# A two-layer decoder trunk: the last three weight blocks ahead of each norm by token half, the norms filled by token half, and GpSimd's rescale in 512-column pieces

## The chip, the core and the metric

The kernel runs on one core of one Trainium2 chip. The metric is the device time of one execution in microseconds (us). The core has five engines with a queue each: TensorE (PE in the profile; its weight loads are PEld), VectorE (DVE), ScalarE (ACT), GpSimd (POOL) and SyncE (SP, which issues the loads). An engine takes its instructions in the order in which they are written; semaphores order the engines against each other.

## What is computed

Two post-norm layers over 256 tokens of 2048 features, in float32. Layer 0 mixes with retention and pooling, layer 1 with sliding-window attention; each is followed by a convolutional gated feed-forward (FFN), and each half ends in a layer norm:

```python
for layer in range(DEPTH):                       # DEPTH = 2
    mix = retention_pool_mixer(...) if layer % 2 == 0 else swa_sink_attention(...)
    x = layer_norm(DEEPNORM_ALPHA * x + mix, ln_gain[layer, 0], ln_bias[layer, 0])
    ffn = conv_glu_ffn(x, ffn_w_in[layer], ffn_conv_w[layer], ffn_conv_b[layer], ffn_w_out[layer])
    x = layer_norm(DEEPNORM_ALPHA * x + ffn, ln_gain[layer, 1], ln_bias[layer, 1])
```

There are four norms: norm 0 (ahead of the FFN of layer 0), norm 1 (ahead of the attention's input projection), norm 2 (ahead of the FFN of layer 1) and the last one, which makes the output. A norm needs mean and variance over all 2048 features of a token, and different tokens do not meet in it.

## The kernel before

**Blocks.** All large products run over 356 weight blocks of 512 x 512 (4 tiles of 128 rows, 512 columns), numbered by `s`. SyncE loads a block into `raw` (4 buffers), ScalarE rounds it to `w_hi` (`high(s)`, L455, 4 buffers), VectorE makes the rest `w_lo = raw - w_hi` (`low(s)`, L698, 3 buffers), and TensorE multiplies. When TensorE has finished a block it counts `used` up. `low(s)` waits until block `s - 3` is used up, `high(s)` until block `s - 4` is. The activations stand as `T` in the same two parts (256 tokens high, 256 low). A product is written one of two ways: turned (`turned_mm`, L1099 and L1100: the weight tile is stationary, tokens stream; 64 pairs of one 512-column and one 256-column matmul for four blocks) or plain (`plain_tile`, L1116 to L1118: 128 tokens are stationary and 512 weight columns stream; 12 matmuls for a token half of a block, 24 for a block).

**Up to a norm.** The last projection of a stage is plain: for each block both token halves `a = 0, 1`, 12 matmuls each. After the last block VectorE adds the result to the residual `xres` (`add_last`, L739), takes statistics (L745, L750), ScalarE the square root (L502), VectorE the reciprocal, and then normalises `xres` in eight pieces of 512 columns (L768: four column quarters, two token halves).

**The fill.** The next product needs the normalised rows turned: TensorE transposes two feature tiles for both token halves (`turn_pair`, L1128, four transposes, two pairs a quarter), ScalarE applies gain and bias and writes `half` (L482, twice) and then the high part of `T` (L487), VectorE writes the low part (L758, `fill_normed_low`) and counts `t_ready`. There are eight such pairs for a norm. `first_chunk` on TensorE turns quarter 0, and then, between the two parts of each block's product, the whole quarter that the next block needs. A part is the product with two feature tiles: 8 pairs of matmuls. "Chunk 0" below is the first four blocks after a norm, "chunk 1" the next four, `base` the first block's number.

**The rescale.** The residual needs gain, bias and the factor alpha as well. GpSimd waits until the eighth pair is turned (`turned`) and then runs four instructions of 2048 columns on `xres`: two multiplications (L428) and two additions (L431). Later residual additions, the load of the next norm's parameters, and in the attention the reuse of the parameters' buffer wait for its count `scaled`.

**Chunk 1 of an FFN.** VectorE's queue holds `low(base+5)`, `low(base+6)`, a small copy, a convolution of two feature tiles (a sum of a PSUM tile and `half`, L719; two scalings, L890; four multiply-adds, L893, all of 256 columns a tile), `low(base+7)`, a second such convolution, `low(base+8)`, `low(base+9)`. Chunk 1 of the attention has the lows and a few small instructions on the keys and values.

**The end.** The last norm (L788 to L805) is divided among VectorE, ScalarE and GpSimd after the last matmul; five transfers store the output (L395 to L403).

Of the kernel before, what the change touches and what calls it, by code (L numbers as in the profile page):

```python
# [20 lines left out]
F32 = mybir.dt.float32  # L21
F32R = mybir.dt.float32r
ALU = mybir.AluOpType
# [48 lines left out]
S_FFN = [S_FFN0, S_FFN1]  # L72

FILL_X, FILL_RET, FILL_LN0, FILL_LN1, FILL_ATT, FILL_LN2 = 0, 8, 12, 20, 28, 36
FILL_LN = [FILL_LN0, FILL_LN1, FILL_LN2]
ATT_FILL_BANKS = [2, 3, 2, 3, 4, 5, 4, 5]
ATT_FILL_AT = {0: 0, 1: 2, 4: 4, 6: 6}

SPLIT_AFTER = {1: 0, 5: 1, 7: 2}
# [43 lines left out]
def build_trunk(nc, x, ln_gain, ln_bias, even_w_in, pool_w, pool_scale, even_w_out, attn_w_qkv, attn_b_qkv,  # L125
# [10 lines left out]
    with ExitStack() as ctx:  # L136
# [142 lines left out]

        ret_bank = lambda hd: 4 + hd % 2  # L280
# [5 lines left out]
        def _(sp):  # L286
# [30 lines left out]
            def ffn(l):  # L317
# [6 lines left out]
                sp.wait_ge(scaled, TOK * (2 * l + 2))  # L324
# [68 lines left out]
            for q in range(2):  # L393
                sp.wait_ge(last_first, q + 1)
                sp.dma_start(out_t[:, 0, cols(2 * q * COLS, 2 * COLS)], xres[:, 0, cols(2 * q * COLS, 2 * COLS)]) \  # L395
                    .then_inc(stored, 16)
            sp.wait_ge(last_second, 1)
            sp.dma_start(out_t[:, 1, cols((NCH - 1) * COLS)], xres[:, 1, cols((NCH - 1) * COLS)]) \
                .then_inc(stored, 16)
            for n0, n1 in ((0, NCH - 2), (NCH - 2, NCH - 1)):  # L400
                c = slice(COLS * n0, COLS * n1)
                sp.wait_ge(last_scaled, n1)
                sp.dma_start(out_t[:, 1, c], xres[:, 1, c]).then_inc(stored, 16)  # L403
# [4 lines left out]
        def _(pool):  # L408
# [11 lines left out]
            for m in range(3):  # L420

                pool.wait_ge(lnp_landed, 32 * (m + 1))
                nc.gpsimd.tensor_scalar(lnp, lnp, ALPHA, 1.0, ALU.mult, ALU.mult).then_inc(pool_step, 1)
                pool.wait_ge(turned, FILL_LN[m] + 8)
# [7 lines left out]
                steps += TOK  # L432
# [13 lines left out]
        def _(act):  # L446
# [26 lines left out]
            def fill_normed(m, s):  # L473

                for j in range(8):
                    n = FILL_LN[m] + j
                    act.wait_ge(turned, n + 1)
                    if j >= 2:
                        act.wait_ge(t_ready, n - 1)
                    for t in range(2):  # L480
                        c = KT * m + 2 * j + t
                        ins = nc.scalar.activation(half[:, n % 2, t], ps[:, fill_bank(n), SEQ * t:SEQ * t + SEQ],  # L482
# [3 lines left out]
                    act.wait_ge(act_step, 8 * m + j + 1)  # L486
                    nc.scalar.activation(T[:, 2 * j:2 * j + 2, 0:SEQ], half[:, n % 2], ACT.Copy).then_inc(t_hi, 1)  # L487
                    if j in SPLIT_AFTER:
                        high(s + HI_LEAD + SPLIT_AFTER[j])

# [9 lines left out]
            def ln_root(m):  # L500
                act.wait_ge(var_ready, m + 2)
                nc.scalar.activation(rstd[:], rstd[:], ACT.Sqrt).then_inc(std_ready, 1)  # L502
# [71 lines left out]
            for s in range(S_EVEN_OUT, S_FFN0):  # L574
                high(s + HI_LEAD)
# [12 lines left out]
            def feed_forward(l):  # L588
                base, tp, gp = S_FFN[l], TP_FFN[l], 2 * FC * l
                ln_root(2 * l)  # L590
# [26 lines left out]
                for j in range(16):  # L617
# [30 lines left out]
            ln_root(1)  # L648
            fill_normed(1, S_ODD_IN)
            for s in range(S_ODD_IN + 1, S_FFN1):  # L650
# [19 lines left out]
            ln_root(3)  # L670

            act.wait_ge(shift_ready, 1)
            for n in range(NCH):
                c = slice(COLS * n, COLS * n + COLS)
                nc.scalar.activation(xres[:, 1, c], xres[:, 1, c], ACT.Identity, bias=shift[:], scale=rstd[:, 1:2]) \
                    .then_inc(last_normed, 1)


        @block.vector
        def _(dve):  # L680
# [49 lines left out]
            def add_last(m, bank, count_in, ended):  # L730

                n = NCH - 1
                c = slice(COLS * n, COLS * n + COLS)
                for a in range(TOK):
                    if a == 0:
                        dve.wait_ge(last_half, m + 1)
                    else:
                        dve.wait_ge(used, ended)
                    ins = vec.tensor_tensor(xres[:, a, c], xres[:, a, c], ps[:, bank + a], ALU.add)  # L739
                    if a == TOK - 1:  # L740
                        ins.then_inc(count_in[0], 1)
                        dve.wait_ge(*count_in)
                    else:
                        chain(ins)
                    ins = vec.bn_stats(stats[:, a, n], xres[:, a, c])  # L745
                chain(ins)

            def inverse_root(m):
                for a in range(TOK):
                    ins = vec.bn_aggr(mean_var[:, a], stats[:, a])  # L750
                chain(ins)
                vec.tensor_scalar(rstd[:], mean_var[:, :, 1], EPS, None, ALU.add).then_inc(var_ready, 1)
                dve.wait_ge(std_ready, m + 2)
                chain(vec.reciprocal(rstd[:], rstd[:]))

            def fill_normed_low(n, j):
                dve.wait_ge(t_hi, n + 1)
                vec.tensor_tensor(T[:, 2 * j:2 * j + 2, SEQ:2 * SEQ], half[:, n % 2],  # L758
                                  T[:, 2 * j:2 * j + 2, 0:SEQ].bitcast(F32), ALU.subtract).then_inc(t_ready, 1)

            def layer_norm(m, s):

                inverse_root(m)

                def normalise(q):
                    for a in range(TOK):
                        c = slice(COLS * q, COLS * q + COLS)
                        ins = vec.tensor_scalar(xres[:, a, c], xres[:, a, c], mean_var[:, a, 0:1],  # L768
                                                rstd[:, a:a + 1], ALU.subtract, ALU.mult)
                    ins.then_inc(ln_chunk, 1)  # L770

                for q in range(3):
                    normalise(q)
                for j in range(8):
                    fill_normed_low(FILL_LN[m] + j, j)
                    if j == 0:
                        normalise(3)
                    if j == 1 and m == 1:
                        low(s + LO_LEAD - 1)
                    if j in SPLIT_AFTER:  # L780
# [707 lines left out]
```

## Time and profile before

| | us |
|---|---|
| median of three runs | 2164.05 (2163.34 to 2165.15) |
| span of the profiled execution | 2162.8 |
| TensorE busy | 2097.6 (97%) |
| VectorE busy | 1455.7 (67%) |
| ScalarE busy | 902.5 (42%) |
| GpSimd busy | 90.6 (4%) |
| mean granted TensorE clock | 0.985 of full speed |

The span is the profiled execution from its first to its last instruction, 1.25 us less than the median of the timed runs. Busy time is a sum over an engine's instructions; TensorE's matmuls overlap at their ends. PEclk is the granted TensorE clock as a share of the full 2.4 GHz, so 0.50 is 1.2 GHz. A row of a timeline that ends in x2 stands for two instructions one after the other, with their time from the first start to the last end.

### The profile page before, as it was taken

Reading aid. Unit: us, or ns where it says so; the run is one execution under the profiler, and the core shown is the slowest. Engines: PE = TensorE matmul, PEld = TensorE weight load, DVE = VectorE, ACT = ScalarE, POOL = GpSimd, SP = SyncE. Lnnn points to the kernel's source line nnn. Section 1 sums busy time; section 2 is a strip of 40 time slices with the busy share of each in tenths; the row PEclk is TensorE's granted clock in tenths of the full one; section 3 lists DMA queues with packets and bytes.
Section 4 is the critical chain, followed back from the end, with each engine's and each line's share of the span. In section 5 each row is a group of like instructions: output and inputs, shape, how many; then the busy total and the mean of one; then the engine's idle time right before and its main releaser. Section 6 shows DMA issues by size and latency. Waiting matters only on the chain.

```text
span 2162.8 us, 27677 instructions
## 1 busy us (share of the span) xinstructions
PE 2097.6 (97%) x10996; PEld 1788.2 (83%) x10996; DVE 1455.7 (67%) x1564; ACT 902.5 (42%) x852; POOL 90.6 (4%) x29
## 2 busy tenths in 40 slices
PE   8999998999999999999989999989999999999996
PEld 7888887788888888888877888778888888888885
DVE  5434455967766667767777666586776767767677
ACT  4443435434433434434443554444343334434341
POOL 0000000200000000000003000030000000000001
PEclk9999999999999999999999999999999999999998
DMA  8664373565555555555544335446555555555551
GB/s 303 221 194 156 114 260 133 196 206 183 192 178 192 193 191 178 193 191 180 176 160 161 118 117 179 153 156 233 179 189 194 180 190 193 175 195 193 192 178 58
DMA packets 194077, 390.39 MB, mean 180 GB/s; under 512 B 6409, under 2 KB 8803, under 8 KB 192995
## 3 DMA queue, kind: packets, MB, share of 16 engines
q1 hardware_dynamic: 193731, 389.31, 53.7%
q8 instruction: 42, 0.69, 0.1%
q10 hardware_dynamic: 288, 0.26, 0.1%
q14 instruction: 16, 0.13, 0.0%
HBM read 387.18 MB, written 2.10 MB: 180 GB/s over the span
## 4 chain that ended last, share of the span: by engine, by line
PE 95%; DVE 3%; ACT 1%; issue 0%; DMA 0%; DVEq 0%; ACTq 0%
PE ps L1099 36%; PE ps L1100 18%; PE ps L1116 12%; PE ps L1118 12%; PE ps L1117 12%; DVE w_lo L698 1%; DVE T L758 1%; PE ps L1128 1%; PE ps L1382 1%; PE ps L1365 0%; PE ps L1247 0%; DVE xres L798 0%; ACT w_hi L455 0%; PE ps L1358 0%; PE ps L1356 0%
## 5 line engine op out<-in xcount | busy, mean ns | idle before, releaser
L1099 PE MATMUL ps<-T,w_hi 128*128 128x512 f32 x3360 | 1205.9, 403 | 26.0 <-DVE T L758 13.9
L698 DVE TENSOR_TENSOR w_lo<-raw,w_hi 128x2048 fp32r<-128x2048 f32 x355 | 839.9, 2368 | 460.8 <-PE ps L1100 350.2
L455 ACT ACTIVATE w_hi<-raw 128x2048 fp32r<-128x2048 f32 x355 | 680.7, 1919 | 1041.9 <-PE ps L1100 626.2
L1100 PE MATMUL ps<-T,w_lo 128*128 128x256 f32 x3360 | 951.3, 283 | 0.0
L1099 PEld LDWEIGHTS ps<-T,w_hi 128*128 128x128 f32 x3360 | 640.0, 190 | 188.2 <-DVE T L758 17.0
L1100 PEld LDWEIGHTS ps<-T,w_lo 128*128 128x128 f32 x3360 | 644.2, 192 | 0.7
L1116 PE MATMUL ps<-w_hi,gT 128*128 128x512 f32 x672 | 262.3, 390 | 0.0
L1118 PE MATMUL ps<-w_hi,gT 128*128 128x512 f32 x672 | 262.0, 390 | 0.0
L1117 PE MATMUL ps<-w_lo,gT 128*128 128x512 f32 x672 | 261.8, 390 | 0.0
L1116 PE MATMUL ps<-w_hi,T 128*128 128x512 f32 (+1 forms) x512 | 199.0, 389 | 0.7 <-DVE T L712 0.7
L1118 PE MATMUL ps<-w_hi,T 128*128 128x512 f32 (+1 forms) x512 | 197.0, 385 | 0.0
L1117 PE MATMUL ps<-w_lo,T 128*128 128x512 f32 (+1 forms) x512 | 196.9, 385 | 0.0
L893 DVE SCALAR_TENSOR_TENSOR arena<-arena,cur 128x256 f32<-128x256 f32 x352 | 155.1, 482 | 6.3
L724 DVE TENSOR_TENSOR xres<-xres,ps 128x1024 f32<-128x1024 f32 x92 | 112.0, 1218 | 70.0 <-PE ps L1118 69.9
L1118 PEld LDWEIGHTS ps<-w_hi,gT 128*128 128x128 f32 x672 | 126.2, 188 | 26.7
L1116 PEld LDWEIGHTS ps<-w_hi,gT 128*128 128x128 f32 x672 | 126.2, 188 | 26.4
L1117 PEld LDWEIGHTS ps<-w_lo,gT 128*128 128x128 f32 x672 | 126.2, 188 | 25.6
L1116 PEld LDWEIGHTS ps<-w_hi,T 128*128 128x128 f32 x512 | 97.2, 190 | 21.5 <-issue 1.3
L1118 PEld LDWEIGHTS ps<-w_hi,T 128*128 128x128 f32 x512 | 97.0, 190 | 19.0
L1117 PEld LDWEIGHTS ps<-w_lo,T 128*128 128x128 f32 x512 | 97.1, 190 | 18.2
L719 DVE TENSOR_TENSOR arena<-ps,half 128x512 f32<-128x512 f32 x96 | 65.7, 688 | 17.3 <-ACT half L497 12.1
L890 DVE TENSOR_SCALAR arena<-arena,cur 128x256 f32<-128x256 f32 x176 | 64.7, 410 | 3.2
(126 smaller groups left out, 811.9 us busy)
## 6 DMA issues: line engine op xcount, KB each, us to landing
raw<-ffn_w_in SPq DMA_DIRECT2D x176, 1024.0 KB, 5.0
raw<-ffn_w_out SPq DMA_DIRECT2D x88, 1024.0 KB, 5.0
raw<-even_w_in SPq DMA_DIRECT2D x39, 1024.0 KB, 5.2
raw<-attn_w_qkv SPq DMA_DIRECT2D x20, 1024.0 KB, 5.2
raw<-even_w_out SPq DMA_DIRECT2D x16, 1024.0 KB, 5.1
raw<-attn_w_out SPq DMA_DIRECT2D x16, 1024.0 KB, 5.0
arena<-ln_gain SPq DMA_DIRECT2D x4, 1024.0 KB, 7.2
arena<-ln_bias SPq DMA_DIRECT2D x4, 1024.0 KB, 9.2
```

Source lines behind the costliest of these rows:

```text
L455: nc.scalar.activation(w_hi[:, s % HI], raw[:, s % RAW], ACT.Copy).then_inc(hi_ready, 1)
L698: vec.tensor_tensor(w_lo[:, s % LO], raw[:, s % RAW], w_hi[:, s % HI].bitcast(F32), ALU.subtract).then_inc(lo_ready, 1)
L719: vec.tensor_tensor(to, ps[:, bank:bank + 2, 0:SEQ], half[:, n % 2], ALU.add).then_inc(added, 1)
L724: vec.tensor_tensor(xres[:, :, c], xres[:, :, c], ps[:, bank:bank + 2], ALU.add).then_inc(count_in, 1)
L758: vec.tensor_tensor(T[:, 2 * j:2 * j + 2, SEQ:2 * SEQ], half[:, n % 2], T[:, 2 * j:2 * j + 2, 0:SEQ].bitcast(F32), ALU.subtract).then_inc( ...
L890: ins = vec.tensor_scalar(conv[:, i], h[:, i, 0:SEQ], cur[:, kind, 0, i:i + 1], cur[:, kind, 3, i:i + 1], ALU.mult, ALU.add)
L893: ins = vec.scalar_tensor_tensor(conv[:, i], h[:, i, k:k + SEQ], cur[:, kind, k, i:i + 1], conv[:, i], ALU.mult, ALU.add)
L1099: mm(ps[:, bank], w_hi[:, s % HI, k, c], T[:, t], start=kg == 0 and k == 0, stop=False)
L1100: return mm(ps[:, bank, 0:SEQ], w_lo[:, s % LO, k, c], T[:, t, 0:SEQ], start=False, stop=kg == KG - 1 and k == GK - 1)
L1116: mm(ps[:, bank, 0:n], x_hi, w_hi[:, s % HI, k, c], start=start and k == 0, stop=False)
L1117: mm(ps[:, bank, 0:n], x_hi, w_lo[:, s % LO, k, c], start=False, stop=False)
L1118: ins = mm(ps[:, bank, 0:n], x_lo, w_hi[:, s % HI, k, c], start=False, stop=stop and k == GK - 1)
```

## The change

- **Ends by token half.** The last three blocks ahead of each norm (`ENDS = 3`) run for tokens 0 to 127 first (`ends_first`), then for 128 to 255 (`ends_second`). `used` is counted only in the second pass. Norms 0 to 2 put the transposes of three units of the first half between the matmuls of the second pass.
- **Norm by token half.** VectorE adds, takes statistics and normalises the first half (`first_half_norm`), then the second (`second_half_norm`).
- **Fill in 12 units** (`LN_UNITS`): three of four tiles of half 0, eight of two tiles of half 1, and the last four tiles of half 0 as unit 7. A unit of half 1 has two transposes where a pair had four. `norm_chunk` takes the place of `first_chunk` for the norms.
- **Rescale.** GpSimd runs 16 instructions of 512 columns instead of four of 2048, and waits for `used` to reach `SCALE_AFTER` too: the end of chunk 0 for the two FFNs, two blocks into chunk 0 for the attention. The scaling of the parameters goes from one instruction to four.
- **The last norm.** The first half is normed during the second pass, half of its columns by ScalarE and GpSimd; the second half by VectorE alone, and the stores follow in that order.

The core of the diff:

```diff
+SCALE_AFTER = [S_FFN0 + KG, S_ODD_IN + 2, S_FFN1 + KG]
+LN_UNITS = [(0, 0, 4), (0, 4, 8), (0, 8, 12), (1, 0, 2), (1, 2, 4), (1, 4, 6), (1, 6, 8), (0, 12, 16),
+            (1, 8, 10), (1, 10, 12), (1, 12, 14), (1, 14, 16)]
+PAIR_UNIT = [3, 4, 5, 6, 8, 9, 10, 11]
+END_TURNS = {4: 0, 5: 1, 7: 2}
-SPLIT_AFTER = {1: 0, 5: 1, 7: 2}
+BLOCK_AFTER = {4: 1, 6: 2, 9: 3, 11: 4}
...
-                for a in range(TOK):
-                    nc.gpsimd.tensor_tensor(xres[:, a], xres[:, a], lnp[:, 0], ALU.mult).then_inc(pool_step, 1)
-                for a in range(TOK):
-                    pool.wait_ge(pool_step, steps + a + 1)
-                    nc.gpsimd.tensor_tensor(xres[:, a], xres[:, a], lnp[:, 1], ALU.add).then_inc(scaled, 1)
+                pool.wait_ge(turned, FILL_LN[m] + LN_FILLS)
+                pool.wait_ge(used, SCALE_AFTER[m])
+                pieces = [(a, slice(COLS * n, COLS * n + COLS)) for a in range(TOK) for n in range(NCH)]
+                for a, c in pieces:
+                    nc.gpsimd.tensor_tensor(xres[:, a, c], xres[:, a, c], lnp[:, 0, c], ALU.mult) \
+                        .then_inc(pool_step, 1)
+                for a, c in pieces:
+                    steps += 1
+                    pool.wait_ge(pool_step, steps)
+                    nc.gpsimd.tensor_tensor(xres[:, a, c], xres[:, a, c], lnp[:, 1, c], ALU.add).then_inc(scaled, 1)
...
+            def second_half_norm(m, s):
+                variance(m, 1)
+                inverse_root(m, 1)
+                normalise(1, 0)
+                fill_normed_low(m, 2)
+                for q in range(1, NCH):
+                    normalise(1, q)
+                for u in range(3, LN_FILLS):
+                    fill_normed_low(m, u)
+                    if u in BLOCK_AFTER:
+                        low(s + BLOCK_AFTER[u])
...
+            def norm_chunk(s0, m, product):
+                first = FILL_LN[m]
+                turn_unit(m, 3)
+                turn_unit(m, 4)
+                for j in range(8):
+                    kg, part = divmod(j, 2)
+                    pe.wait_ge(t_ready, first + PAIR_UNIT[j] + 1)
+                    if part == 0:
+                        ready(s0 + kg)
+                    for k in (2 * part, 2 * part + 1):
+                        ins = product(s0 + kg, kg, k)
+                    if part == 1:
+                        ins.then_inc(used, 1)
+                    if 5 + j < LN_FILLS:
+                        turn_unit(m, 5 + j)
```

**TensorE, chunk 0 after norm 0, before.** L1128 are the transposes of a quarter, L1099 and L1100 the matmul pairs of the product. The quarter that is turned here is needed from the row that waits for `lo_ready,t_ready`.

```order
L1128 MATMUL ps<-ident,xres 128x128 [waits t_ready,ln_chunk]
L1128 MATMUL ps<-ident,xres 128x128 x7
L1099 MATMUL ps<-T,w_hi 128x512 [waits t_ready]
L1100 MATMUL ps<-T,w_lo 128x256
...
L1099 MATMUL ps<-T,w_hi 128x512 [waits lo_ready,t_ready]
```

Between the transposes and the first matmul that needs them stand the eight pairs of one part.

**TensorE, the same chunk, after**: L1214 are a unit's transposes, L1147 and L1148 the pairs. The first two rows here are unit 8, then comes part 4, then unit 9, then part 5.

```order
L1214 MATMUL ps<-ident,xres 128x128 [waits t_hi,ln_chunk]
L1214 MATMUL ps<-ident,xres 128x128
L1147 MATMUL ps<-T,w_hi 128x512 [waits lo_ready,t_ready]
L1148 MATMUL ps<-T,w_lo 128x256
...
L1214 MATMUL ps<-ident,xres 128x128 [waits t_hi,ln_chunk]
L1214 MATMUL ps<-ident,xres 128x128
L1147 MATMUL ps<-T,w_hi 128x512 [waits t_ready]
L1148 MATMUL ps<-T,w_lo 128x256
```

By `PAIR_UNIT` parts 4 to 7 wait for units 8 to 11, and each of these is turned right behind the part before: nothing stands between a unit's transposes and the matmul that waits for it. Units 5 and 6 have a part between.

**VectorE, the end of the fill and the head of chunk 1, after.** L779 are low parts of `T`, L719 is `low` (from `low(base+3)` on), L740, L910 and L913 the convolution. The order of these instructions is that of before.

```order
L719 TENSOR_TENSOR w_lo<-raw,w_hi 128x2048 [waits used,hi_ready]
L779 TENSOR_TENSOR T<-half,T 128x2x128 [waits t_hi] x2
L719 TENSOR_TENSOR w_lo<-raw,w_hi 128x2048 [waits used,hi_ready]
L924 MEMSET arena 128x4x2
L719 TENSOR_TENSOR w_lo<-raw,w_hi 128x2048 [waits used,hi_ready,dve_step]
L719 TENSOR_TENSOR w_lo<-raw,w_hi 128x2048 [waits used,hi_ready]
L928 COPY cur<-taps 128x16
L740 TENSOR_TENSOR arena<-ps,half 128x2x256 [waits half_out,dve_step]
L910 TENSOR_SCALAR arena<-arena,cur 128x256 [waits added]
L910 TENSOR_SCALAR arena<-arena,cur 128x256
L913 SCALAR_TENSOR_TENSOR arena<-arena,cur 128x256 [waits dve_step]
```

What moved is the unit before `low(base+4)`: it is now the unit that TensorE's last part of chunk 0 waits for.

**GpSimd, the rescale of norm 0, after.**

```order
L443 TENSOR_TENSOR xres<-xres,arena 128x512 [waits pool_step,used,turned]
L443 TENSOR_TENSOR xres<-xres,arena 128x512 x7
L448 TENSOR_TENSOR xres<-xres,arena 128x512 [waits pool_step] x8
```

The first piece now waits for `used` as well; before, `turned` alone let it go.

## Rows read from the trace of the kernel before

**Rows 1.** The page's groups: `low` and `high` (busy us, mean ns, idle before).

```profile
L698 DVE TENSOR_TENSOR w_lo<-raw,w_hi 128x2048 fp32r<-128x2048 f32 x355 | 839.9, 2368 | 460.8 <-PE ps L1100 350.2
L455 ACT ACTIVATE w_hi<-raw 128x2048 fp32r<-128x2048 f32 x355 | 680.7, 1919 | 1041.9 <-PE ps L1100 626.2
```

**Rows 2.** TensorE's waits, whole run: for whom, us in total, times, longest.

```profile
PE ps L1099 <- DVE T L758: 13.9, 9, 2.5
PE ps L1128 <- DVE xres L768: 10.8, 3, 3.6
PE ps L1099 <- DVE w_lo L698: 10.8, 3, 3.6
```

**Rows 3.** Busy time by stretch, norms 0 and 1, and the end (length, engines, PEclk, DMA, GB/s).

```profile
341.60:347.00 5.40, 5.37 (x24) 4.13 (x22) 3.67 (x3) 3.21 (x2) 0.00 (x0) 1.00 0.58 195
347.00:354.20 7.20, 1.98 (x9) 1.58 (x9) 5.68 (x14) 2.64 (x6) 0.00 (x0) 0.64 0.18 71
354.20:359.30 5.10, 5.10 (x16) 4.33 (x17) 3.71 (x4) 2.56 (x3) 0.00 (x0) 0.50 0.11 12
...
373.30:386.60 13.30, 10.31 (x48) 8.05 (x47) 12.00 (x3) 6.38 (x8) 13.23 (x3) 0.87 0.24 79
386.60:390.20 3.60, 0.00 (x0) 0.01 (x1) 3.56 (x3) 2.88 (x3) 3.60 (x2) 0.97 0.00 0
390.20:393.40 3.20, 3.18 (x10) 2.72 (x11) 3.20 (x1) 0.00 (x0) 3.20 (x1) 0.50 0.67 207
...
1148.50:1154.60 6.10, 6.07 (x19) 5.23 (x20) 6.10 (x1) 0.00 (x0) 4.31 (x1) 0.50 0.51 172
...
2142.70:2162.80 20.10, 0.00 (x0) 0.00 (x0) 14.82 (x17) 3.13 (x5) 9.56 (x6) 0.63 0.26 104
```

**Rows 4.** Timeline of TensorE, norm 0 (start, length, instruction, idle before).

```profile
350.58 1.97 PE L1128 MATMUL ps<-ident,xres 128*128 128x128 f32 x8 [3.61 <-DVE xres L768]
...
371.55 0.39 PE L1099 MATMUL ps<-T,w_hi 128*128 128x512 f32 x1
...
371.89 0.40 PE L1099 MATMUL ps<-T,w_hi 128*128 128x512 f32 x1
...
372.24 1.04 PE L1128 MATMUL ps<-ident,xres 128*128 128x128 f32 x8
```

**Rows 5.** Timeline of VectorE and ScalarE behind the last matmul of norm 0.

```profile
349.52 2.82 DVE L768 TENSOR_SCALAR xres<-xres,mean_var,rstd 128x512 f32<-128x512 f32 x6
...
351.73 1.02 ACT L482 ACTIVATE half<-ps,ln_cols 128x256 f32<-128x256 f32 x2 [2.44 <-PE ps L1128]
352.78 0.63 ACT L487 ACTIVATE T<-half 128x512 fp32r<-128x512 f32 x1
...
353.44 0.69 DVE L758 TENSOR_TENSOR T<-half,T 128x512 fp32r<-128x512 f32 x1 [1.10 <-ACT T L487]
```

**Rows 6.** Timeline of GpSimd during the rescale of norm 0.

```profile
373.37 9.57 POOL L428 TENSOR_TENSOR xres<-xres,arena 128x2048 f32<-128x2048 f32 x2 [95.47 <-PE ps L1128]
382.90 11.61 POOL L431 TENSOR_TENSOR xres<-xres,arena 128x2048 f32<-128x2048 f32 x2
```

**Rows 7.** The same stretch on VectorE.

```profile
374.60 8.89 DVE L758 TENSOR_TENSOR T<-half,T 128x512 fp32r<-128x512 f32 x2 [1.96 <-ACT T L487]
383.41 6.66 DVE L698 TENSOR_TENSOR w_lo<-raw,w_hi 128x2048 fp32r<-128x2048 f32 x1
```

**Rows 8.** The end: pieces of 512 columns on GpSimd.

```profile
2149.48 1.71 POOL L439 TENSOR_TENSOR xres<-xres,arena 128x512 f32<-128x512 f32 x1
...
2152.82 1.71 POOL L439 TENSOR_TENSOR xres<-xres,arena 128x512 f32<-128x512 f32 x1
```

**Rows 9.** The last two stores on SyncE's queue.

```profile
2158.47 0.94 SPq L403 DMA_DIRECT2D out<-xres  x2
```

**Rows 10.** TensorE alone in two stretches (busy, PEclk, DMA share, GB/s).

```profile
1270.60:1274.00 3.40, 2.09 (x19) 1.00 0.89 280
...
345.60:349.00 3.40, 1.37 (x7) 1.00 0.77 283
```

More of the change, by code:

```diff
@@ L748, in inverse_root @@
[L748 to L780, printed above, removed]
-                        low(s + LO_LEAD + SPLIT_AFTER[j])
@@ L956, in feed_forward @@
                 tail, c = base + FFN_GROUPS - 4 * KG, FC - 1
-                for j in range(16):
+                for j in range(13):
                     if j == 11:
@@ L1160, in first_chunk, with turn_unit @@
                     ins.then_inc(used, 1)
+            def turn_unit(m, u):
+                a, t0, t1 = LN_UNITS[u]
+                n = FILL_LN[m] + u
+                pe.wait_ge(ln_chunk, TOK * NCH * m + NCH * a + t0 // KG + 1)
+                if u >= 4:
+                    pe.wait_ge(t_hi, n - 3)
+                for t in range(t0, t1):
+                    i = t - t0
+                    ins = nc.tensor.transpose(ps[:, fill_bank(n), P * i:P * i + P], xres[:, a, P * t:P * t + P],
+                                              ident[:])
+                ins.then_inc(turned, 1)
@@ new lines, in ends_first, with ends_second @@
+            def ends_first(blocks, each):
+                for s, src, tile, bank, start, stop in blocks:
+                    ready(s)
+                    ins = plain_tile(s, src, tile, bank, 0, start, stop)
+                    if each or stop and s == blocks[-1][0]:
+                        ins.then_inc(last_half, 1)
+            def ends_second(blocks, m):
+                for i, (s, src, tile, bank, start, stop) in enumerate(blocks):
+                    for k in range(GK):
+                        ins = plain_tile(s, src, tile, bank + 1, 1, start, stop, only=k)
+                        if k == GK - 1:
+                            ins.then_inc(used, 1)
+                        if m is not None and GK * i + k in END_TURNS:
+                            turn_unit(m, END_TURNS[GK * i + k])
@@ L1259, in projection @@
                     ins = plain_tile(s, gT if in_g else T, 0 if in_g else GK * kg, bank + a, a, first, last)
-                    if a == 0 and last and n == NCH - 1:
-                        ins.then_inc(last_half, 1)
                 ins.then_inc(used, 1)
-            for i in range(NCH * KG):
+            for i in range(NCH * KG - ENDS):
                 s, n, pos = S_EVEN_OUT + i, i // KG, i % KG
@@ L1438, in _ @@
                 scores(b)
+            ends = [(S_FFN1 - ENDS + i, T, GK * (1 + i), ODD_OUT_BANKS[-1], False, i == ENDS - 1)
+                    for i in range(ENDS)]
+            ends_first(ends, False)
+            ends_second(ends, 2)
             feed_forward(1)
```

301 lines of the change are left out of this document (179 added, 122 removed).

## The prediction, made before the changed kernel was run

> **What bounds the kernel now.** TensorE is busy 97% of the span, so time goes where it waits or runs at half clock. I read its waits first [rows 2], then a table of stretches around the norms [rows 3], then the timelines there. The three norms 0 to 2 look alike. Behind the last matmul TensorE has nothing for 3.6 us, does eight transposes and waits again; the first matmul comes after 7.2 us [rows 3, 4]. Near the end of chunk 0 it loses 3.0 us (13.30 less 10.31 busy) and at the head of chunk 1 another 3.6, 10.8 over the three norms [rows 2, 3]. After each such hole the granted clock is 0.50, so that 5.1 us behind the norm give half their work, and 3.2 (norm 0) or 6.1 (norm 1) at chunk 1 [rows 3]. At the end 20.1 us pass without a matmul [rows 3].
>
> The two later holes come from GpSimd. While its four instructions run (21.2 us together), one `low` lasts 6.66 us instead of 2.3, and two small fills 8.89 together instead of 1.4 [rows 1, 5 to 7]: the two engines take turns, an instruction each. Take out what VectorE did in between, two fills and a `low`. VectorE's pace is (2.37 - 0.69)/1536 = 1.1 ns a column [rows 1, 5], so 0.56 for 512 columns, 2.2 for 2048, 0.28 for 256. That leaves 21.2 - 3.3 = 17.9 us of GpSimd's own, **1.11 us for 512 columns**. The end agrees: two pieces and two VectorE instructions of 512 in 3.34 us [rows 8], 1.67 - 0.56 = 1.11.
>
> **The change part by part.** The sum runs from the last three blocks to the end of chunk 1, norm by norm. Paces: 12 plain matmuls take 2.7 us (24 in 5.40, rows 3), a turned pair 0.345 [rows 4], so a part 2.8, a block 5.5, a chunk 22.1; a transpose takes 0.13 [rows 4].
>
> *Ends.* The matmuls are the same. Three blocks' first halves take 8.2 us, the last `low` among them starts with the first of them and is needed 5.4 us later: it fits. Twelve transposes go in (+1.56) and eight fewer stand in chunk 0 (-1.04): +0.5 a norm, **+1.6**. The first half's add, statistics and norm (2.5 + 1.9, rows 3 and 5), the next `low` and two fills fit the 9.7 us of the second pass; TensorE covers them.
>
> *The gap.* Behind the last matmul VectorE still adds, takes statistics and normalises one piece: 3.0 us instead of 3.6 [rows 4, 5]. Four transposes at half clock take 1.0. VectorE meanwhile has a fill (0.69) and three pieces (1.4) and then the first unit's low part (0.42): first matmul at 5.6. Against 7.2 that is 1.6 less at norms 0 and 2. At norm 1 VectorE's queue also holds the second half's other two adds and statistics, one pair of them behind a `low`, so that the last add starts 1.2 us late: 6.8, which I count as no gain. **-3.2** together. I found no reason for the half clock behind it to shorten: the hole is still above 4 us, and 1.37 us busy of 3.4 was followed by 0.50, 2.09 of 3.4 was not [rows 10].
>
> *Round trips in chunk 0.* Parts 4 to 7 wait for a unit turned just ahead of them. ScalarE writes two tiles (1.02 for 256 columns each, rows 5; its pace is (1.92 - 0.63)/1536 = 0.84 ns a column [rows 1, 5], so 0.81) and copies 256 columns (0.42), VectorE subtracts (0.42), and four hand-overs take 0.2: 1.85 us in which TensorE is idle. Halving all of today's trip gives 1.4, all of it 2.6. I take 1.85: the parts have rows. Four a norm, twelve in all: **+22.2** (16 to 31). Nothing covers them. Before, a part (2.8 us) stood between, and there was no wait.
>
> *Clock there.* Holes of 1.85 between parts of 2.8. In 3.4 us that leaves about 1.4 us busy, close to the stretch that was followed by half clock [rows 10]. I take one fall a norm at the price seen in chunk 0 today, 0.87 over 13.3 us, that is 1.7 us: **+5.1** (0 to 15).
>
> *Rescale out of chunk 0.* Its 3.0 us of waits and 1.7 of clock go: **-14.0** for three norms. Its waits at chunk 1's head go too, 10.8, and their clock, 1.6 at norm 0 and 3.0 at norms 1 and 2: **-18.4**.
>
> *Rescale in chunk 1 (norms 0 and 2).* GpSimd's 16 pieces are 17.9 us, now from the end of chunk 0. Four blocks later, at 22.1 us, TensorE needs `low(base+8)`. Ahead of it on VectorE stand: the rest of `low(base+4)` (0.9, since the unit before it comes late: ScalarE's 1.9 us and the 2.3 of `low` start 0.5 us before the last part, which lasts 2.8), four lows (8.8), four scalings, a copy (together 0.8) and eight multiply-adds (2.2). With strict turns each of these 16 or 17 lets a piece in, so all 16 pieces come first: 17.9 + 12.7 = 30.6 less 22.1 is 8.5; I take 8.1, some of VectorE's starts overlapping. TensorE waits at `base+4` (0.9), `base+7` (2.5) and `base+8` (4.7). Twice: **+16.2**. Clock: two falls, 1.7 and 2.3: **+8**. Bounds: if only instructions known to wait count (two inputs in SBUF), 12 pieces get in and 3.7 us are left a norm; if GpSimd gets few turns, only the 0.9.
>
> The Trainium skill, SBUF — State Buffer, "Who interferes with whom", says that one read and write port pair is shared, is held for the whole instruction, and that two-port forms of tensor_scalar and copy take it as well as two-input instructions. The turns agree with [rows 6, 7]; that the scalings count no run here shows. By it 16 pieces come ahead.
>
> *Norm 1.* The rescale may start two blocks into chunk 0, so `turned` lets it go, with the last unit's transposes, 4.6 us ahead of the end of chunk 0. The second piece stands ahead of that unit's fill (0.95 more), and turns make `low(base+4)` and `low(base+6)` late by 0.7 together. There is no convolution, so a low meets one piece and fits into a block: 2.2 + 1.1 of 5.5. `scaled` is complete some 31 us after the start, about 3 us behind the eighth block. VectorE waits there, and TensorE's first scores need what stands behind that wait 5.5 us after the eighth block: covered by half a microsecond. **+1.7**; if that cover goes, 1 to 3 more.
>
> *End.* Before, 20.1 us [rows 3]. After: the first half's add starts 8.2 us before the last matmul, its statistics and root take 2.5, and its four instructions of 512 columns 2.8 and, since GpSimd's four pieces take turns with them, 1 to 2 more; behind them two adds with statistics of 1.45 each. So VectorE comes to the last add 2.0 us after the last matmul. From there 2.5 to the first normed piece, eight instructions of 512 columns at 0.69 [rows 5] 5.5, and one store; today the last store starts 3.9 us before the span's end (2158.47 and half of 0.94, against 2162.8) [rows 9]. 2.0 + 2.5 + 5.5 + 3.9 = 13.9: **-6.2**. If GpSimd's turns cost nothing it is 12, if they cost twice as much 15.5.
>
> Sum: +1.6 - 3.2 + 22.2 + 5.1 - 14.0 - 18.4 + 16.2 + 8 + 1.7 - 6.2 = **+13.0**. The span becomes 2162.8 + 13.0 = 2175.8; it stands 1.25 under the median before, and I keep that: 2177.
>
> **The rivals.** *Faster: turns without a price in chunk 1.* If VectorE's short instructions pass in groups and GpSimd fits its pieces into VectorE's other time, 7.2 us of the 8.1 and the 4 of clock go at each FFN norm: 13.0 - 22.4 = -9.4, 2155. It decides when fewer than 9 pieces stand ahead of `low(base+8)`: 12.7 + 8.5 x 1.11 = 22.1. For it: nothing is known of turns with 0.3 us instructions. Against it: every pair in [rows 6 to 8] alternates. *Half of that:* scalings and copy do not take a turn, 12 pieces: 13.0 - 8.8 - 4 = 0, 2164. *Round trips hidden:* if the order of transposes did not bind, 27.3 go: 2150. The order of the queue speaks against it. *Slower still: the clock.* If TensorE falls to 1.2 GHz after most of the round trips, three falls a norm, +10: 2187. The Trainium skill, TensorE: Matmul & The Clock Gate, "Part 4: PE-mode transpose", says that transposes do not count as busy; the clock was 0.50 during the eight in the gap [rows 3, 4], which does not separate the causes. By that rule this rival gains.
>
> **How the numbers follow.** Forecast (2169 to 2183) 0.55; slower still 0.11; half 0.10; no price in chunk 1 0.15; trips hidden or another gain 0.09. Slower by over 0.2% (4.3 us, about what a measurement of this kernel can tell) 0.66, within 0.11, faster 0.23. The range leaves out the 0.09 and part of the two ends: 2154 to 2187.
>
> **What would show it.** In chunk 0, four holes of 1.85 us a norm before L1147 for `T`; in chunk 1 of the FFNs, waits of L1147 for `w_lo` of 8 us together while GpSimd's pieces last 1.4 to 3.3 us each; no such waits in chunk 0; a first matmul 5.6 us after a norm; 14 us after the last matmul. If the holes in chunk 0 are missing the forecast is wrong by 27 us; if `w_lo` is in time in chunk 1, by 22.

## The result

Four runs of each kernel, timed in turns.

| | before | after |
|---|---|---|
| median, us | 2163.7 (2163.0 to 2165.15) | 2180.84 (2179.83 to 2181.58) |
| ratio after / before, 95% interval | | 1.0074 (1.0062 to 1.0085) |
| span of the profiled execution, us | 2162.8 | 2178.9 |

The change makes the kernel 0.7% slower: 17.1 us by the medians, 16.1 by the spans. 2177 was predicted, in a range of 2154 to 2187, slower with a chance of 0.66. The time between the last matmuls of the stages, read from TensorE's timeline:

| stage, us | before | after | difference |
|---|---|---|---|
| start to norm 0 | 346.97 | 347.63 | +0.7 |
| norm 0 to norm 1 (FFN) | 758.8 | 769.7 | +10.9 |
| norm 1 to norm 2 (attention) | 277.0 | 280.3 | +3.2 |
| norm 2 to the last matmul (FFN) | 759.9 | 768.8 | +8.9 |
| behind the last matmul | 20.1 | 12.5 | -7.6 |

### The profile page after: what moved, and what is told of

Read it like the earlier page. It is cut to its first block, busy times and chain, and to the rows that moved or that the text cites. A ratio compares the mean times of both kernels' runs of the same rounds, so it can differ in the third digit from the quotient of the medians.

```text
span 2178.9 us, 27743 instructions
## 1 busy us (share of the span) xinstructions
PE 2106.8 (97%) x10996; PEld 1792.2 (82%) x10996; DVE 1445.1 (66%) x1590; ACT 915.9 (42%) x914; POOL 115.8 (5%) x72
## 4 chain that ended last, share of the span: by engine, by line
PE 92%; DVE 5%; ACT 1%; issue 1%; DMA 0%; DVEq 0%; ACTq 0%
PE ps L1147 35%; PE ps L1148 18%; PE ps L1164 12%; PE ps L1166 12%; PE ps L1165 12%; DVE w_lo L719 1%; DVE arena L913 1%; PE ps L1481 1%; ACT half L500 0%; DVE T L779 0%; PE ps L1464 0%; PE ps L1214 0%; PE ps L1176 0%; DVE arena L910 0%; DVE xres L772 0%
## 5 line engine op out<-in xcount | busy, mean ns | idle before, releaser
L1147 PE MATMUL ps<-T,w_hi 128*128 128x512 f32 x3360 | 1213.1, 405 | 41.7 <-DVE T L779 27.4
L719 DVE TENSOR_TENSOR w_lo<-raw,w_hi 128x2048 fp32r<-128x2048 f32 x355 | 823.8, 2323 | 459.9 <-PE ps L1148 342.2
L1148 PE MATMUL ps<-T,w_lo 128*128 128x256 f32 x3360 | 952.1, 283 | 0.0
L1147 PEld LDWEIGHTS ps<-T,w_hi 128*128 128x128 f32 x3360 | 642.5, 191 | 207.5 <-DVE T L779 31.2
L1148 PEld LDWEIGHTS ps<-T,w_lo 128*128 128x128 f32 x3360 | 645.7, 192 | 0.7
L913 DVE SCALAR_TENSOR_TENSOR arena<-arena,cur 128x256 f32<-128x256 f32 x352 | 170.6, 526 | 6.3
L745 DVE TENSOR_TENSOR xres<-xres,ps 128x1024 f32<-128x1024 f32 x88 | 107.1, 1218 | 60.8 <-PE ps L1166 60.8
L443 POOL TENSOR_TENSOR xres<-xres,arena 128x512 f32<-128x512 f32 x24 | 42.5, 1802 | 901.5 <-PE ps L1214 707.3
L740 DVE TENSOR_TENSOR arena<-ps,half 128x512 f32<-128x512 f32 x96 | 65.7, 688 | 17.6 <-ACT half L517 12.5
```

The lines of the kernel that those rows point to most:

```text
L443: nc.gpsimd.tensor_tensor(xres[:, a, c], xres[:, a, c], lnp[:, 0, c], ALU.mult) \
L719: vec.tensor_tensor(w_lo[:, s % LO], raw[:, s % RAW], w_hi[:, s % HI].bitcast(F32), ALU.subtract).then_inc(lo_ready, 1)
L740: vec.tensor_tensor(to, ps[:, bank:bank + 2, 0:SEQ], half[:, n % 2], ALU.add).then_inc(added, 1)
L745: vec.tensor_tensor(xres[:, :, c], xres[:, :, c], ps[:, bank:bank + 2], ALU.add).then_inc(count_in, 1)
L913: ins = vec.scalar_tensor_tensor(conv[:, i], h[:, i, k:k + SEQ], cur[:, kind, k, i:i + 1], conv[:, i], ALU.mult, ALU.add)
L1147: mm(ps[:, bank], w_hi[:, s % HI, k, c], T[:, t], start=kg == 0 and k == 0, stop=False)
```

## The profile after

The page, engines: busy us, share, instructions.

```profile
span 2178.9 us, 27743 instructions
PE 2106.8 (97%) x10996; PEld 1792.2 (82%) x10996; DVE 1445.1 (66%) x1590; ACT 915.9 (42%) x914; POOL 115.8 (5%) x72
```

TensorE is as busy in share as before. Busy time hides what matters here: it grew by 9.2 us with the same matmuls, 7.5 of them because more of it is at half clock (the account below). GpSimd's busy time grew by 25 us. The rescale has the same columns and is 23 of these; a part of that is waiting for its turn inside an instruction.

TensorE's waits in the whole run, as [rows 2].

```profile
PE ps L1147 <- DVE T L779: 27.4, 15, 2.9
PE ps L1147 <- DVE w_lo L719: 13.0, 4, 5.7
PE ps L1214 <- DVE xres L772: 9.7, 3, 3.7
```

The wait for `T` has doubled (13.9 before), that for `w_lo` has grown a little (10.8 before) and has another place. By stretch, as [rows 3]: the gap behind norm 0 and what follows it; a round trip; three stretches of 3.4 us in chunk 0; then chunk 1, its large hole and what follows it; the last trip of norm 1; the end.

```profile
347.60:352.90 5.30, 0.95 (x5) 0.53 (x4) 4.82 (x11) 2.52 (x7) 0.00 (x0) 0.81 0.27 106
352.90:357.70 4.80, 4.76 (x15) 4.08 (x16) 2.71 (x2) 2.45 (x3) 0.00 (x0) 0.50 0.00 0
367.70:369.50 1.80, 0.00 (x0) 0.00 (x1) 0.42 (x1) 1.22 (x3) 0.00 (x0) 1.00 0.80 188
374.80:378.20 3.40, 3.40 (x11) 2.92 (x12) 2.26 (x1) 1.11 (x1) 0.00 (x0) 0.50 0.00 0
381.60:385.00 3.40, 3.40 (x12) 2.90 (x11) 0.00 (x0) 0.00 (x0) 0.00 (x0) 0.50 0.32 122
388.40:391.80 3.40, 3.40 (x13) 2.93 (x12) 2.51 (x3) 3.40 (x3) 0.00 (x0) 0.50 0.00 0
392.70:416.10 23.40, 22.41 (x128) 19.06 (x126) 23.15 (x17) 8.53 (x8) 23.40 (x14) 1.00 0.52 179
416.10:421.70 5.60, 0.00 (x1) 0.00 (x0) 5.60 (x4) 3.26 (x3) 3.43 (x3) 0.77 0.00 0
421.70:426.00 4.30, 4.26 (x13) 3.68 (x14) 4.30 (x2) 1.94 (x3) 0.00 (x0) 0.50 0.74 239
1157.00:1159.90 2.90, 0.03 (x1) 0.00 (x0) 1.53 (x1) 2.80 (x4) 2.78 (x3) 0.99 0.00 0
2166.40:2178.90 12.50, 0.00 (x0) 0.00 (x0) 9.15 (x16) 0.20 (x1) 1.53 (x2) 0.65 0.42 167
```

Read it in four steps. The gap is 5.3 us instead of 7.2. The third row is one of the round trips: nothing on TensorE while ScalarE and VectorE make the unit. The three rows at 0.50 are matmuls at 1.2 GHz inside chunk 0, busy 3.40 of 3.40, at a clock that lets through half of the work. In chunk 1 there is a hole of 5.6 us in which VectorE is busy throughout, and 4.3 us at half clock behind it.

One round trip on TensorE, ScalarE and VectorE (the timeline: start, length, instruction, idle before):

```profile
372.44 0.38 PE L1214 MATMUL ps<-ident,xres 128*128 128x128 f32 x2
372.86 0.81 ACT L500 ACTIVATE half<-ps,ln_cols 128x128 f32<-128x128 f32 x2 [3.87 <-PE ps L1214]
373.69 0.42 ACT L505 ACTIVATE T<-half 128x256 fp32r<-128x256 f32 x1
374.14 0.43 DVE L779 TENSOR_TENSOR T<-half,T 128x256 fp32r<-128x256 f32 x1 [4.70 <-ACT T L505]
374.62 0.68 PE L1147 MATMUL ps<-T,w_hi 128*128 128x512 f32 x1 [1.80 <-DVE T L779]
```

0.81, 0.42 and 0.43 of work and 0.14 in hand-overs are the 1.80 us in which TensorE is idle. Eleven of the twelve trips read 1.80 or 1.81; the last one of norm 1 reads 2.91, where GpSimd runs already.

The head of chunk 1 on GpSimd, VectorE and TensorE, norm 0:

```profile
392.69 13.85 POOL L443 TENSOR_TENSOR xres<-xres,arena 128x512 f32<-128x512 f32 x8 [114.99 <-PE ps L1148]
397.13 1.26 DVE L928 COPY cur<-taps 128x16 f32<-128x16 f32 x1
399.15 1.93 DVE L910 TENSOR_SCALAR arena<-arena,cur 128x256 f32<-128x256 f32 x2
401.11 5.71 DVE L913 SCALAR_TENSOR_TENSOR arena<-arena,cur 128x256 f32<-128x256 f32 x4
406.50 13.03 POOL L448 TENSOR_TENSOR xres<-xres,arena 128x512 f32<-128x512 f32 x8
406.75 3.38 DVE L719 TENSOR_TENSOR w_lo<-raw,w_hi 128x2048 fp32r<-128x2048 f32 x1
412.75 5.65 DVE L913 SCALAR_TENSOR_TENSOR arena<-arena,cur 128x256 f32<-128x256 f32 x4
418.33 5.55 DVE L719 TENSOR_TENSOR w_lo<-raw,w_hi 128x2048 fp32r<-128x2048 f32 x2
421.74 0.79 PE L1147 MATMUL ps<-T,w_hi 128*128 128x512 f32 x1 [5.63 <-DVE w_lo L719]
```

and the same small instructions of VectorE before, at that place, where GpSimd had nothing to do:

```profile
398.79 0.16 DVE L909 COPY cur<-taps 128x16 f32<-128x16 f32 x1
399.71 0.74 DVE L890 TENSOR_SCALAR arena<-arena,cur 128x256 f32<-128x256 f32 x2
400.49 1.80 DVE L893 SCALAR_TENSOR_TENSOR arena<-arena,cur 128x256 f32<-128x256 f32 x4
```

A multiply-add takes 1.4 instead of 0.45 us, a copy of 16 columns 1.26 instead of 0.16. Each lets one whole GpSimd piece in, short or long. The two sums that read a PSUM tile (L740) do not: they take 0.69 and 0.68 us among the pieces, and 0.69 where GpSimd has nothing to do. The 16th piece starts just ahead of `low(base+8)` (418.09 and 418.33), so all 16 pieces delay it, as the prediction had it for strict turns. The Trainium skill, SBUF — State Buffer, "Who interferes with whom", names copy and tensor_scalar, in their two-port forms, among the instructions that take the shared port pair: the trace agrees (1.26 us for the copy, 0.97 as the mean of two scalings).

The end: the last residual add, and the last stores.

```profile
2168.07 0.67 DVE L754 TENSOR_TENSOR xres<-xres,ps 128x512 f32<-128x512 f32 x1
2173.32 3.11 SPq L412 DMA_DIRECT2D out<-xres  x3
```

**An account.** Summing TensorE's rows up to the last matmul gives its idle time, its time busy at half clock, and (busy less half of that) its work in microseconds at full clock. The loss by the clock is half the time at half clock. "Behind" is the time from the last matmul to the end of the span.

| up to the last matmul, us | idle | at half clock | loss by the clock | work at full clock | behind |
|---|---|---|---|---|---|
| before | 45.1 | 42.3 | 21.2 | 2076.5 | 20.1 |
| after | 59.6 | 57.3 | 28.7 | 2078.1 | 12.5 |
| difference | +14.5 | | +7.5 | +1.7 | -7.6 |

## The experiments

Theory: two causes of loss, the round trips with the clock they bring, and the rescale in chunk 1, whose delay is set by the number of turns; the end gives some back. The rivals: the clock would be low anyway; the lateness in chunk 1 comes from columns or from the order on VectorE, not from turns; the late start of the rescale is harmless. Each ratio below is against the kernel before on the same chip, with its 95% interval.

### e1: each unit turned one part earlier

```diff
                     if part == 0:
                         ready(s0 + kg)
+                    if 5 + j < LN_FILLS:
+                        turn_unit(m, 5 + j)
                     for k in (2 * part, 2 * part + 1):
                         ins = product(s0 + kg, kg, k)
...
-                    if 5 + j < LN_FILLS:
-                        turn_unit(m, 5 + j)
```

> The changed kernel with one thing moved: in chunk 0 each unit's transposes stand ahead of a part's product, not behind it, so that a part of 2.8 us lies between them and the matmul that needs them. If the round trips are what costs: the twelve holes of 1.8 us go (21.7 us, and the 1.1 more at norm 1), and with them the nine stretches at half clock inside chunk 0 (about 15 us); the hole in chunk 1 grows by 1 to 2 us a norm, since the rescale then starts earlier against the same queue. 2180.8 - 38 + 3 = 2146. Rival, that the half clock in chunk 0 comes from the transposes or from the gap behind the norm and not from the holes: the falls stay, 2160. Rival, that something else (ScalarE's fills) sets the pace of chunk 0: above 2170.

Measured: 2143.15 us, ratio 0.9904 (0.9888 to 0.9921), 37.7 less than after. The account: idle 38.4, at half clock 26.4, work 2077.1. So 21.2 us of idle time and 15.5 of clock went. The stretch that read 0.79 in after:

```profile
372.00:388.00 16.00, 16.00 (x93) 13.67 (x92) 12.69 (x11) 12.07 (x12) 8.16 (x4) 1.00 0.67 225
```

TensorE's waits:

```profile
PE ps L1147 <- DVE w_lo L719: 14.9, 5, 5.6
PE ps L1214 <- DVE T L779: 4.3, 3, 1.5
```

The waits of the product for `T` have gone; what stays of them is one wait of the transposes a norm. The large hole in chunk 1 is as in after (5.63 at norm 0) and the small one has grown from 0.99 to 1.65, so the two causes are nearly separate. This single move turns the loss into a gain.

### e9: transposes in the holes, to part the trip from its clock

Behind the transposes of each of the four units eight more transposes, of `ident`, go to a PSUM bank that is free; nobody reads them. Nothing is left out.

```diff
+                    if j in (3, 4, 5, 6):
+                        n = first + 5 + j
+                        pe.wait_ge(t_hi, n - 2)
+                        for i in range(8):
+                            nc.tensor.transpose(ps[:, 4 + (n + 1) % 4, P * (i % 4):P * (i % 4) + P],
+                                                ident[:], ident[:])
```

> The changed kernel with eight more transposes of the identity (1.0 us) in each of the four holes of 1.8 us of a chunk 0, so that TensorE is idle for 0.8 us there; when the product goes on is unchanged. Nothing reads what they write. If they keep the clock at 2.4 GHz: the nine stretches at half clock inside chunk 0 go, 2180.8 - 15 = 2166. If transposes do not count for the clock: the falls stay, 2181. Either way the waits for T remain, only their idle share shrinks.

Measured: 2168.47 us, ratio 1.002 (1.001 to 1.003), 12.4 less than after with 96 matmuls more. The stretch around three trips, after and then e9:

```profile
372.00:388.00 16.00, 10.59 (x43) 8.57 (x41) 3.57 (x4) 6.05 (x11) 0.00 (x0) 0.79 0.21 66
```

```profile
372.00:388.00 16.00, 12.78 (x80) 10.71 (x78) 5.72 (x5) 9.46 (x13) 0.28 (x1) 1.00 0.20 66
```

All nine stretches at half clock in chunk 0 are gone: 57.3 us at half clock became 27.4 in the whole run, a gain of 15.0 us. The trips are as long as before; 0.93 us of each is still idle. The kernel gains less than 15, since the 96 transposes add 13.2 us of work and fill only 11.1 of idle time. So of the 37.7 us of e1 some 15 were the clock and the rest the trips themselves. And the transposes did hold the clock up: that speaks against the sentence of the Trainium skill, TensorE: Matmul & The Clock Gate, "Part 4: PE-mode transpose", which the prediction weighed (transposes do not count as busy in the same way). Whether they count in full no run here shows.

### e4: only the pieces, in the kernel before

The kernel before with 16 instructions of 512 columns for the four of 2048 (counts of `scaled` adapted); the start of the rescale, the ends and the fill are as before.

```diff
-                for a in range(TOK):
-                    nc.gpsimd.tensor_tensor(xres[:, a], xres[:, a], lnp[:, 0], ALU.mult).then_inc(pool_step, 1)
...
+                pieces = [(a, slice(COLS * n, COLS * n + COLS)) for a in range(TOK) for n in range(NCH)]
+                for a, c in pieces:
+                    nc.gpsimd.tensor_tensor(xres[:, a, c], xres[:, a, c], lnp[:, 0, c], ALU.mult) \
+                        .then_inc(pool_step, 1)
```

> The kernel before with the third part of the change alone: its rescale in 16 pieces of 512 columns, started where it started before (eighth pair turned). By turns: a fill near the end of chunk 0 waits 1.1 us and not 3.3 to 4.5, so the 3.0 us of holes there and their half clock go; four or five pieces run in VectorE's idle time, the rest meet VectorE in chunk 1 and leave a hole of about 2.5 us at the two FFNs and none at norm 1. 2163.7 - 23 = 2141 (2136 to 2150). Rival, that only the sum of GpSimd's work counts: 2160 to 2164.

Measured: 2138.95 us, ratio 0.9883 (0.9866 to 0.9899). As expected: one part of the change alone is worth 25 us.

```profile
PE ps L1101 <- DVE w_lo L700: 6.6, 4, 1.7
PE ps L1101 <- DVE T L760: 5.3, 3, 2.0
```

Against [rows 2] the wait for `T` fell from 13.9 to 5.3, which are the three waits in the gaps behind the norms, and that for `w_lo` from 10.8 to 6.6. The account: idle 12.7 less, half clock 17.1 instead of 42.3 us, which is 12.6. Half of the gain is the clock behind holes that vanished.

### e11, e8, e6: the start of the rescale

e11 is e4 with the changed kernel's start:

```diff
                 pool.wait_ge(turned, FILL_LN[m] + 8)
+                pool.wait_ge(used, (S_FFN0 + KG, S_ODD_IN + 2, S_FFN1 + KG)[m])
```

> The kernel before with the rescale in 16 pieces of 512 columns (2139 with its start at the eighth pair), and now with the wait for used of the changed kernel too: the FFNs' rescales start when chunk 0 ends. Nothing else of the change is in it. If the late start is what makes the holes in chunk 1: they grow from 3.3 us (1.65 and 1.63) to the 7.3 of the kernel with units turned ahead, and the half clock behind them comes back (3.4 each): 2139 + 2 x (4.0 + 3.4) = 2154. Rival, that the holes in chunk 1 come with the fill by token half (other order, other load on ScalarE): 2139.

Measured: 2144.7 us, ratio 0.9912 (0.9895 to 0.9928), 5.8 more than e4. The direction was right, the size not: 2154 was expected.

```profile
PE ps L1102 <- DVE w_lo L701: 9.1, 2, 4.8
```

One hole of 4.4 to 4.8 us an FFN, where e1 had 7.3 in two. So the late start is not all. In e1 and after VectorE is inside `low(base+5)` when the pieces begin (in e1 since 379.52, the first piece at 379.84); in e11 it is one `low` of 2.3 us further and begins `low(base+6)` then (380.06, the first piece at 380.10). That this explains the whole of the missing 9 us was not tested.

e8 is after without this wait, e6 is e1 without it; each takes out one line:

```diff
                 pool.wait_ge(turned, FILL_LN[m] + LN_FILLS)
-                pool.wait_ge(used, SCALE_AFTER[m])
```

> The changed kernel with the rescale's wait for used taken out alone: it starts with the last unit's transposes, 4.6 us before chunk 0 ends. By turns three or four pieces get in there, so the holes in chunk 1 shrink by 3.5 us at norms 0 and 2, part of their clock goes (1.7 each), and the last round trip is 1 us longer, as at norm 1 in the changed kernel: 2180.8 - 8 = 2173. Rival: no change, 2181.

> Units turned a part ahead, and the rescale without its wait for used: it starts when the last unit is turned, 5.5 us before chunk 0 ends. By turns, about three pieces of 1.1 us then run in chunk 0; the two holes in chunk 1 (1.65 and 5.63 us at norms 0 and 2) shrink by 3.3 together and half of their clock goes: 2143 - 2 x (3.3 + 1.7) = 2133. Rival, that the place of the start doesn't matter: 2143.

Measured: e8 2171.95 us, ratio 1.0034 (1.0019 to 1.0048), 8.9 less than after; e6 2134.83 us, ratio 0.9863 (0.9847 to 0.988), 8.3 less than e1. In e8 and e6:

```profile
PE ps L1146 <- DVE T L778: 29.4, 15, 2.9
PE ps L1146 <- DVE w_lo L718: 4.5, 3, 1.6
```

```profile
PE ps L1146 <- DVE w_lo L718: 10.3, 7, 2.6
```

The wait for `used` costs 8 to 9 us with the round trips and without them. What it protects, the last unit of chunk 0, costs less unprotected: in e8 the last trip of every norm is 2.9 us instead of 1.8.

### e2 and e5: pieces of 256 columns

```diff
-SCALED = [TOK + TOK * NCH * m for m in range(4)]
+SCALED = [TOK + 2 * TOK * NCH * m for m in range(4)]
...
-                pieces = [(a, slice(COLS * n, COLS * n + COLS)) for a in range(TOK) for n in range(NCH)]
+                pieces = [(a, slice(COLS // 2 * n, COLS // 2 * n + COLS // 2)) for a in range(TOK) for n in range(2 * NCH)]
```

e2 is after with this, e5 is e1 with it.

> The changed kernel with the rescale in 32 pieces of 256 columns in place of 16 of 512. If VectorE and GpSimd take strict turns, an instruction each, VectorE's 16 instructions ahead of low(base+8) let in 16 pieces of 0.56 us (9 us) and not 17.9 us: the holes of 6.5 us in chunk 1 of the two FFNs shrink to 1 or less and their half clock goes, 2181 - 17 = 2164. Rival, that the sum of GpSimd's work has to fit into chunk 1 however it is cut: no change or a little more, 2181 to 2184.

> Both edits: units turned a part ahead, rescale in 32 pieces of 256 columns. If the two causes add up: 2146 - 17 - 3 (the growth of the hole goes too) = 2126 to 2130, which beats both kernels. If they share a cause, 2140 or more.

Measured: e2 2173.87 us, ratio 1.0041 (1.0029 to 1.0052), between the two expectations; e5 2138.05 us, ratio 0.988 (0.9864 to 0.9897), where 2126 to 2130 was expected. TensorE's waits in e2, and GpSimd's timeline:

```profile
PE ps L1147 <- DVE T L779: 26.4, 15, 1.8
PE ps L1164 <- DVE gT L938: 6.1, 2, 3.4
PE ps L1481 <- DVE arena L1112: 2.8, 1, 2.8
PE ps L1147 <- DVE w_lo L719: 0.8, 2, 0.6
```

```profile
392.71 17.68 POOL L443 TENSOR_TENSOR xres<-xres,arena 128x256 f32<-128x256 f32 x16 [114.78 <-PE ps L1148]
410.36 21.05 POOL L448 TENSOR_TENSOR xres<-xres,arena 128x256 f32<-128x256 f32 x16
```

and the copy on VectorE that took 1.26 us in after:

```profile
396.59 0.71 DVE L928 COPY cur<-taps 128x16 f32<-128x16 f32 x1
```

Turns by instruction, not by column, are shown: an instruction of VectorE now waits about half as long, and the same columns in half-size pieces cut the wait for `w_lo` from 13.0 to 0.8. But the theory forgot what follows. The rescale now ends at 431.4 instead of 419.5, and VectorE is late once more: for the gated product `gT` (L938) behind chunk 2, 3.4 and 2.7 us in the two FFNs, and in the attention for the scores, behind the wait for `scaled` (2.8). The holes moved; in e2 7 us were gained, in e5 5. The size in e2 is less firm than the others: its ten times run from 2165.33 to 2176.52, with a mean granted clock from 0.990 down to 0.982, and the trace is of an execution of 2175.98.

### e7: e1 with the rescale by token half

All columns of token half 0 are turned with unit 7, so its pieces may start there, half 1 behind the last unit; there is no wait for `used`.

```diff
-                pool.wait_ge(turned, FILL_LN[m] + LN_FILLS)
-                pool.wait_ge(used, SCALE_AFTER[m])
...
+                for a in range(TOK):
+                    pool.wait_ge(turned, FILL_LN[m] + (8, LN_FILLS)[a])
+                    pieces = [(a, slice(COLS * n, COLS * n + COLS)) for n in range(NCH)]
```

> Units turned a part ahead, and the rescale by token half: the eight pieces of tokens 0 to 127 start when unit 7 is turned, a quarter into chunk 0, the other eight when the last unit is turned. VectorE has idle time in chunk 0, so eight pieces run there: the holes in chunk 1 (7.3 us a norm at norms 0 and 2, and their 3.4 us of clock) go, 2143 - 21 = 2122; up to 5 more if the fills' waits for a piece (1.1 us) outgrow the part that covers them. Rival: the pieces only carry the wait from chunk 1 into chunk 0, 2135 or more.

Measured: 2129.38 us, ratio 0.9841 (0.9825 to 0.9858), the fastest kernel here: 34 us under before, 51 under after. 2122 was expected.

```profile
PE ps L1215 <- DVE T L780: 10.7, 6, 2.0
PE ps L1215 <- DVE xres L773: 9.7, 3, 3.7
```

No wait for `w_lo` is left in chunk 1. A new one of 2.0 us a norm stands in chunk 0, where a unit's transposes wait for VectorE, which now has a `low` and GpSimd's pieces ahead of it: 6 of the missing 7 us. The account: idle 30.0, at half clock 14.0 us. Against e4 (2138.95) it gains 9.6, of which 7.6 is the shorter end.

### e10: the `low` in that place one unit sooner

e10 is e7 with this line changed, too:

```diff
-BLOCK_AFTER = {4: 1, 6: 2, 9: 3, 11: 4}
+BLOCK_AFTER = {4: 1, 6: 2, 8: 3, 11: 4}
```

> The kernel with units turned a part ahead and the rescale by token half (2129), with low(base+3) one unit sooner on VectorE and high(base+3) on ScalarE, behind unit 8 in place of unit 9. In the former, unit 9's low part stands behind that low and behind three pieces of GpSimd's, and TensorE waits 2.0 us for it once a norm. If that order is the cause, these three holes go: 2129.4 - 6 = 2123. Rival, that the turns with GpSimd alone make the hole: it moves to another unit, 2128 to 2130.

Measured: 2129.86 us, ratio 0.9841 (0.9825 to 0.9858), no difference from e7: the rival was right.

```profile
PE ps L1215 <- DVE T L780: 8.1, 6, 1.6
PE ps L1148 <- DVE w_lo L720: 2.4, 3, 0.9
```

The hole of 2.04 at norm 0 became one of 1.21 and one of 0.89. That order alone was not the cause; other orders were not tried.

## Why the prediction was right, step by step

The forecast was right in sign, and the mechanisms of its large terms were found where it said. In size it was 4 us short, and that it was no more is partly luck: the clock in the round trips cost 10.1 us more than put, the holes of chunk 1 and the clock behind them 6.5 less. The measured column sums idle time and loss by the clock over the stretches that a term names, in both traces; the first row is what the others leave. Term by term, in us:

| term | predicted | measured |
|---|---|---|
| ends and gap | -1.6 | +0.1 (what the other rows leave) |
| round trips | +22.2, and 0.95 at norm 1 | +22.8 |
| clock in the round trips | +5.1 | +15.2 |
| waits removed (chunk 0, head of chunk 1) | -19.8 | -19.5 |
| clock removed with them | -12.6 | -12.6 |
| holes in chunk 1 of the FFNs | +16.2 | +13.0 |
| clock behind these | +8 | +4.7 |
| chunk 1 at norm 1 | +0.7 | 0 |
| end | -6.2 | -7.6 |
| sum | +13.0 | +16.1 |

- **The gap** was predicted at 5.6, 6.8 and 5.6 us and is 5.3, 6.0 and 5.3; the half clock behind it stayed, as said. The gaps are 4.2 us shorter together, so the ends must cost about 1 us a norm more than the 0.5 predicted; work at full clock grew by 1.7 in all, with the same number of matmuls. No experiment looked at this remainder, and its cause is open.
- **Round trips**: mechanism, places, number and length as predicted; e1 shows that they are the order of the queue.
- **Clock in the round trips** is the mis-sized term. The prediction took one fall a norm at 1.7 us; there were three, at 1.7 us each ((3.40 at 0.50) / 2), nine in all. The 15.2 lie just outside its own bounds (0 to 15). Its rival "slower still: the clock" named exactly this; its 2187 was missed because chunk 1 came out cheaper. e9 shows that the clock is lost because the holes are empty: with about a microsecond of work in each it stays at 1.00. [rows 10] show what came behind single holes, and no row of before had such a series, so "one fall" was a choice and not worked out. In each norm half clock came behind the second, the third and the fourth hole, though each (1.8 us) is shorter than the holes of before that had it behind them (2.5 and 3.6).
- **Holes in chunk 1**: 6.6 and 6.4 instead of 8.1. Strict turns held, with all 16 pieces in front. What did not come is the 0.9 for `low(base+4)`: the last part of chunk 0 ran at half clock (388.40 to 391.80) and was long enough to cover it. e9, which keeps the trips but not that half clock, bears this out. There TensorE does wait for `low(base+4)` (0.63 us, at 388.20), and it starts on `low(base+8)` 30.5 us behind GpSimd's first piece (387.72 to 418.18), 8.4 over the 22.1 of a chunk, where 8.1 were predicted; in after it is 29.05 (392.69 to 421.74). So a part of the two errors is one: the underestimated clock paid for 1.4 us of the overestimated hole. The clock behind the holes was mis-sized too, since only one of the two holes (5.6 us) was followed by half clock.
- **Norm 1**: the last trip grew to 2.9 by a GpSimd piece, as predicted; the holes in chunk 1 did not come. The cover of half a microsecond for the scores held, and went in e2 (2.8 us).
- **The end** was 12.5 instead of 13.9. VectorE came to the last add 1.7 us behind the last matmul (2.0 predicted). From there to its last instruction's end it took 8.0, as predicted (2.5 and 5.5); what was mis-sized is the last store, 2.8 us from there to the end of the span (2176.07 to 2178.9) where 3.9 was put.
- **The rivals on the faster side** fell: neither did short instructions pass in groups (a 0.16 us copy took 1.26), nor were scalings and copy exempt. That the round trips come from the order of the queue, and could not hide, e1 shows.
- **Removed waits**: e4 confirms the two removed terms by themselves. Its waits and its clock together gave 25.3 us by the account; the prediction's -32.4 is for a rescale that is gone from these places altogether, and e4 still has 6.6 us of waits for `w_lo` in chunk 1.

## What to carry to other kernels

Where two engines share a port by turns, the delay that one puts on the other is the number of turns times the length of one of its instructions; count only the instructions that take a turn. So cut the long ones, but see what comes behind them, since the total gets longer (e2). In an in-order queue put at least one piece of independent work between making something and using it: e1 moved two lines and gained 37.7 us. And price a series of short holes with the clock that follows it: here it added two thirds of the holes' own length.

## What the runs showed of the hardware

- **Four holes of 1.8 us between the parts of chunk 0** brought TensorE to 1.2 GHz for 3.4 us three times a norm, behind the second, third and fourth, though no hole there was longer than 2.9 us. A single hole of 2.0 us a norm in that place (e7), or two of 1.2 and 0.9 (e10), did not.
- **Transposes hold the clock up**: eight float32 ones, about 1.0 us, in each hole removed all nine falls (e9).
- **VectorE and GpSimd alternate strictly, one instruction each**, however short VectorE's is (0.16 us of copy became 1.26), and tensor_scalar and copy from SBUF take part in it. A sum with one input in PSUM does not (L740, 0.69 us either way).
- **A turn costs VectorE less than GpSimd's instruction lasts**: 1.1 us for a piece of 512 columns (1.26 less 0.16), while pieces with nothing of VectorE's between them, at the end of norm 1's rescale (1184.98 to 1190.02), follow each other every 1.26 us.
